# A fused two-block transformer kernel: rotary angles for 32 rates only, low-rank blocks multiplied with raw x, squares summed on TensorE, and the r product made to follow its operand by tiles

## The reference

```
hn = x * rsqrt(mean(x*x, features) + 1e-6) * g              # per token, g per feature
p  = hn @ w_in                                              # r, k, v, two low-rank blocks, and more
p  = p + (token_shift(p) - p) * mu                          # mix with the token before
r, k, v, wd, ad, gd = split(p)                              # wd, ad: 64 columns each; gd: 128
w  = -softplus(-(w0 + tanh(wd) @ w2)) - 0.5;  a = sigmoid(a0 + ad @ a2);  g = sigmoid(gd) @ g2
angle = position * 10000 ** (-i / 32), i = 0..31            # rotary: 32 rates, for retention later
```

## Time and profile before

| | us |
|---|---|
| median of 3 runs | 2716.07 (2714.88 to 2716.72) |
| the profiled execution: its time | 2714.77 |
| the profiled execution: its span in the trace | 2712.6 |
| PE busy, share of the span | 2498.0 (92%) |
| DVE busy | 1208.9 (45%) |
| POOL busy | 741.4 (27%) |
| ACT busy | 717.4 (26%) |

### The profile page before, as it was taken

The page is one execution under the profiler, slowest core; times in us unless marked ns, Lnnn a source line. Parts: engine busy times, 40 slices in busy tenths (PEclk is TensorE's granted clock), DMA queues, the critical chain, the costliest instruction groups (busy, mean ns, idle before and its releaser), DMA issues.

```text
span 2712.6 us, 33501 instructions
## 1 busy us (share of the span) xinstructions
PE 2498.0 (92%) x12944; PEld 1998.6 (74%) x12944; DVE 1208.9 (45%) x1324; ACT 717.4 (26%) x1013; POOL 741.4 (27%) x375
## 2 busy tenths in 40 slices
PE   3999999999999997998996999999999995999896
PEld 3787877877887886877784788888878774777674
DVE  7543263335335344554516444444421417536633
ACT  3422222131222222223213222222222323014421
POOL 3321221131212110003334333333334443222132
PEclk9999999999999998998996999999999996999988
DMA  2111111121121116434511111111132220111011
GB/s 115 62 55 55 63 49 52 47 71 47 48 70 47 60 50 202 137 105 145 196 47 62 62 46 46 46 46 46 46 132 93 93 93 13 45 48 47 24 35 65
DMA packets 48787, 191.02 MB, mean 70 GB/s; under 512 B 5424, under 2 KB 6192, under 8 KB 47408
## 3 DMA queue, kind: packets, MB, share of 16 engines
q1 hardware_dynamic: 28224, 102.77, 11.4%
q10 hardware_dynamic: 20464, 86.76, 8.8%
HBM read 152.81 MB, written 36.70 MB: 70 GB/s over the span
## 4 chain that ended last, share of the span: by engine, by line
PE 82%; DVE 9%; DVEq 4%; ACT 2%; issue 1%; DMA 1%; POOL 0%; ACTq 0%; POOLq 0%; SPq 0%
PE psg L338 11%; PE psg L334 11%; PE psg L339 11%; PE psg L437 5%; PE psg L442 5%; PE psg L444 5%; PE psg L750 1%; PE psa L402 1%; PE psg L754 1%; PE psg L753 1%; PE psa L533 1%; PE psg L363 1%; PE psg L811 1%; PE psb L522 1%; PE psg L806 1%
## 5 line engine op out<-in xcount | busy, mean ns | idle before, releaser
L271 POOL CAST whi<-wraw 128x1024 fp32r<-128x1024 f32 (+1 forms) x152 | 175.0, 1151 | 1711.3 <-PE psg L437 619.2
L334 PE MATMUL psg<-xhi,whi 128*128 128x512 f32 x1280 | 506.8, 396 | 8.5 <-DVE fg L1204 3.8
L338 PE MATMUL psg<-xlo,whi 128*128 128x512 f32 x1280 | 509.0, 398 | 0.0
L339 PE MATMUL psg<-xhi,wlo 128*128 128x512 f32 x1280 | 505.0, 395 | 0.0
L273 POOL TENSOR_TENSOR wlo<-wraw,whi 128x1024 fp32r<-128x1024 f32 (+1 forms) x152 | 403.4, 2654 | 21.8
L334 PEld LDWEIGHTS psg<-xhi,whi 128*128 128x128 f32 x1280 | 240.5, 188 | 72.1 <-issue 5.9
L338 PEld LDWEIGHTS psg<-xlo,whi 128*128 128x128 f32 x1280 | 240.7, 188 | 58.1 <-issue 1.0
L339 PEld LDWEIGHTS psg<-xhi,wlo 128*128 128x128 f32 x1280 | 240.7, 188 | 57.0
L444 PE MATMUL psg<-xhi,wlo 128*128 128x512 f32 x640 | 265.8, 415 | 0.0
L442 PE MATMUL psg<-xlo,whi 128*128 128x512 f32 x640 | 265.6, 415 | 0.0
L437 PE MATMUL psg<-xhi,whi 128*128 128x512 f32 x640 | 265.4, 415 | 0.0
(11 more groups left out here) (415 smaller groups left out, 4332.9 us busy)
## 6 DMA issues: line engine op xcount, KB each, us to landing
wraw<-w SPq DMA_DIRECT2D x196, 512.0 KB, 3.5
later_scratch<-stage ACTq DMA_DIRECT2D x40, 512.0 KB, 2.7
xres<-xt ACTq DMA_DIRECT2D x4, 1024.0 KB, 11.1
RV<-later_scratch ACTq DMA_DIRECT2D x4, 1024.0 KB, 12.9
RG<-later_scratch ACTq DMA_DIRECT2D x4, 1024.0 KB, 5.1
later_scratch<-rstage ACTq DMA_DIRECT2D x8, 512.0 KB, 2.7
mgr<-later_scratch ACTq DMA_DIRECT2D x8, 512.0 KB, 3.6
mgt<-later_scratch ACTq DMA_DIRECT2D x8, 512.0 KB, 4.4
```

Source lines behind the costliest of these rows:

```text
L271: pool.tensor_copy(whi[:, u, 0:width], wraw[:, u, 0:width])
L334: mm = pe.matmul(psg[b][:, cols], whi[:, slot, w_cols], rhs_hi(k, cols), start=(k == 0), stop=False)
L338: pe.matmul(psg[b][:, cols], whi[:, slot, w_cols], rhs_lo(k, cols), start=False, stop=False)
L339: mm = pe.matmul(psg[b][:, cols], wlo[:, slot, w_cols], rhs_hi(k, cols), start=False, stop=(k == kts - 1))
```

## The change: what it does

- The angles are computed on [128, 256] tiles: 32 rates on 32 partitions, four quarters of the tokens on the four groups of partitions. DVE computes both angle tables ahead of all else, and ACT takes four sines [128, 256] before it touches x. The table in DRAM is written by four transfers and read back by four in place of one and one.
- Positions (a quarter as many) and parameters are loaded ahead of x.
- ACT makes `rhi`, the high half of x times the gain g, as the tiles land, DVE makes `rlo`. The two low-rank blocks are multiplied with these, without the root.
- The squares (ACT makes five, DVE three) are no longer added up by POOL and DVE. TensorE sums each tile's square over partitions and accumulates in PSUM (`square_sums`: the eight one-column matmuls, once for each of the eight tiles).
- Once the root has been spread, DVE copies it to `xrs`, multiplies each low-rank block out of PSUM by it (`low_scaled`), and scales and splits x as before.
- The r product of each pair takes the operand tile by tile with both halves of a tile together, and waits for each tile (`norm_split`).

The diff, cut to its core:

```diff
@@ -45,7 +45,11 @@
-SPLIT_BEFORE = {"yrw": 0, "yret": 4, "merged": 12, "cat": 20}
+SPLIT_BEFORE = {"x": 0, "yrw": 8, "yret": 12, "merged": 20, "cat": 28}
+SQUARED_BY_DVE = (2, 4, 6)
+QT = T // 4
@@ -147,13 +151,16 @@
-        pa_sq = tiles("pa_sq", 8, [P, 2, T])
-        pa_acc = tiles("pa_acc", 10, [P, T])
...
+        pa_sq = tiles("pa_sq", 8, [P, 4, T])
+        pa_tmp = tiles("pa_tmp", 8, [P, 2, T])
+        pa_rstd, xrs = tiles("pa_rstd", 10, [P, T]), tiles("xrs", 11, [P, T])
+        rlo, rhi = tiles("rlo", 12, [P, KT, T], F32R), tiles("rhi", 20, [P, KT, T], F32R)
+        PRE = [tiles("pre_low0", 12, [P, T]), tiles("pre_low1", 13, [P, T])]
+        LOW = [tiles("low0", 14, [P, T]), tiles("low1", 15, [P, T])]
@@ -287,15 +294,6 @@
-            pool.memset(pp[:, 14:15], 1.0)
-            pool.memset(pa_acc[:, :], 0.0)
-            pool.drain()
...
-            for j in range(KT // 2):
-                pool.drain()
-                pool.wait_ge(sem("a_sq"), j + 1)
-                pool.tensor_tensor(pa_acc[:, :], pa_acc[:, :], pa_sq[:, j % 2, :], ALU.add
-                                   ).then_inc(sem("a_added"), 1)
@@ -415,11 +413,54 @@
+            def low_part(u, k, begins=False):
+                for half in range(2):
+                    cols = slice(half * HALF, (half + 1) * HALF)
+                    w_cols = slice(k * P, (k + 1) * P)
+                    mm = pe.matmul(psg[u][:, cols], whi[:, u, w_cols], rhi[:, k, cols], start=(k == 0), stop=False)
+                    if begins and half == 0:
+                        mm.then_inc(w_used, 1)
+                    pe.matmul(psg[u][:, cols], whi[:, u, w_cols], rlo[:, k, cols], start=False, stop=False)
+                    mm = pe.matmul(psg[u][:, cols], wlo[:, u, w_cols], rhi[:, k, cols],
+                                   start=False, stop=(k == KT - 1))
+                if k == KT - 1:
+                    mm.then_inc(g_full, 1)
+            def square_sums(k):
+                if k in SQUARED_BY_DVE:
+                    pe.wait_ge(sem("normed"), SQUARED_BY_DVE.index(k) + 1)
+                else:
+                    pe.wait_ge(sem("a_sq"), k + 1 - sum(j < k for j in SQUARED_BY_DVE))
+                for c in range(NB):
+                    mm = pe.matmul(psa[:, 0, c:c + 1], pa_sq[:, k % 4, c * P:c * P + P], pp[:, 14:15],
+                                   start=(k == 0 and c == 0), stop=(k == KT - 1 and c == NB - 1))
+                mm.then_inc(sem("a_added") if k < KT - 1 else sem("norm_tot"), 1)
+            def low_ready(u):
+                pe.wait_ge(w_ready, B_LORA + u + 3)
+                pe.wait_ge(g_free[u], T_LORA // 2 + 1)
+            low_ready(0)
+            pe.wait_ge(sem("pp_ready"), 1)
+            for k in range(KT):
+                pe.wait_ge(sem("op_split"), SPLIT_BEFORE["x"] + k + 1)
+                low_part(0, k, begins=(k == 0))
+                if k == KT // 2:
+                    low_ready(1)
+                if k >= KT // 2:
+                    low_part(1, k - KT // 2)
+                if k:
+                    square_sums(k - 1)
+            square_sums(KT - 1)
+            for k in range(KT // 2, KT - 2):
+                low_part(1, k, begins=(k == KT // 2))
...
-            norm_factor(pa_acc, pa_rstd, "a")
-            streamed(B_LORA, T_LORA, sem("norm_split"), 0, early=4)
+            pe.wait_ge(sem("norm_exp"), NORM["a"] + 1)
+            spread(pa_rstd).then_inc(sem("norm_rep"), 1)
+            for k in range(KT - 2, KT):
+                low_part(1, k)
@@ -453,7 +494,21 @@
-                for j in range(3):
+                pe.wait_ge(w_ready, B_RW + RW_B * i + 3)
+                pe.wait_ge(g_free[0], 8 * i + 2)
+                for k in range(KT):
+                    pe.wait_ge(sem("norm_split"), k + 1)
+                    w_cols = slice(k * P, (k + 1) * P)
+                    for half in range(2):
+                        cols = slice(half * HALF, (half + 1) * HALF)
+                        mm = pe.matmul(psg[0][:, cols], whi[:, 0, w_cols], xhi[:, k, cols], start=(k == 0), stop=False)
+                        if half == 0 and k == 0:
+                            mm.then_inc(w_used, 1)
+                        pe.matmul(psg[0][:, cols], whi[:, 0, w_cols], xlo[:, k, cols], start=False, stop=False)
+                        mm = pe.matmul(psg[0][:, cols], wlo[:, 0, w_cols], xhi[:, k, cols],
+                                       start=False, stop=(k == KT - 1))
+                mm.then_inc(g_full, 1)
+                for j in range(1, 3):
@@ -899,17 +954,21 @@
...
+            def normed(j):
+                stt(pa_tmp[:, j % 2, :], xres[:, j, :], par_col("g_mix_pre", j), flat(psa), MUL, MUL
+                    ).then_inc(sem("normed"), 1)
+            def normed_low(j):
+                v.wait_ge(sem("norm_high"), j + 1)
+                tt(xlo[:, j, :], pa_tmp[:, j % 2, :], xhi[:, j, :].bitcast(F32), SUB).then_inc(sem("norm_split"), 1)
+                v.drain()
+            def low_scaled(u):
+                v.wait_ge(g_full, u + 1)
+                tt(PRE[u][:, :], psg[u][:, :], xrs[:, :], MUL).then_inc(g_free[u], 1)
@@ -942,33 +1004,41 @@
-            v.wait_ge(sem("a_added"), KT // 2 + 2)
-            for j in range(KT // 2, KT):
-                v.drain()
-                v.wait_ge(sem("a_sq"), j + 1)
-                tt(pa_acc[:, :], pa_acc[:, :], pa_sq[:, j % 2, :], ADD).then_inc(sem("a_added"), 1)
+            v.drain()
+            turns(0.25, rot[:, 1, :])
+            for j in range(KT):
+                v.wait_ge(sem("op_high"), SPLIT_BEFORE["x"] + j + 1)
+                stt(rlo[:, j, :], xres[:, j, :], par_col("g_mix_pre", j), rhi[:, j, :].bitcast(F32), MUL, SUB
+                    ).then_inc(sem("op_split"), 1)
+                if j in SQUARED_BY_DVE:
+                    if j >= 4:
+                        v.wait_ge(sem("a_added"), j - 3)
+                    tt(pa_sq[:, j % 4, :], xres[:, j, :], xres[:, j, :], MUL).then_inc(sem("normed"), 1)
...
-            split_normed("x", xres, "g_mix_pre", pa_rstd, pa_tmp)
+            v.tensor_copy(xrs[:, :], flat(psa))
+            v.drain()
+            low_scaled(0)
+            v.wait_ge(sem("rot_stored"), 64)
+            for j in range(KT):
+                normed(j)
+                if j:
+                    normed_low(j - 1)
+                if j == 3:
+                    low_scaled(1)
+            normed_low(KT - 1)
...
+                stt(LOW[u][:, 1:T], PRE[u][:, 0:T - 1], par_col("mu_low", u), LOW[u][:, 1:T], MUL, ADD
+                    ).then_inc(sem("low_mix"), 1)
@@ -1387,45 +1457,49 @@
...
+            s.wait_ge(sem("angle"), 2)
+            act(rot[:, 2, :], rot[:, 0, :], ACT.Sin)
+            act(rot[:, 3, :], rot[:, 1, :], ACT.Sin)
+            act(rot[:, 0, :], rot[:, 0, :], ACT.Sin, scale=-1.0)
+            act(rot[:, 1, :], rot[:, 1, :], ACT.Sin).then_inc(sem("sincos"), 1)
...
-                s.wait_ge(sem("a_added"), j + 1)
-                act(pa_sq[:, j % 2, :], xres[:, j, :], SQ).then_inc(sem("a_sq"), 1)
+                act(rhi[:, j, :], xres[:, j, :], IDN, scale=par_col("g_mix_pre", j)).then_inc(sem("op_high"), 1)
+                if j not in SQUARED_BY_DVE:
+                    if j >= 4:
+                        s.wait_ge(sem("a_added"), j - 3)
+                    act(pa_sq[:, j % 4, :], xres[:, j, :], SQ).then_inc(sem("a_sq"), 1)
+            s.wait_ge(sem("sincos"), 1)
+            for q in range(4):
+                s.dma_start(rot_d[:, :, q * QT:(q + 1) * QT], rot[q * 32:q * 32 + 32, :, :]
+                            ).then_inc(sem("rot_stored"), 16)
...
+            for u in range(2):
+                s.wait_ge(g_free[u], 2)
+                act(LOW[u][:, :], PRE[u][:, :], IDN, scale=pp[:, 10 + u:11 + u]).then_inc(sem("low_a"), 1)
+            s.wait_ge(sem("low_mix"), 1)
+            act(LOW[0][0:CH, :], LOW[0][0:CH, :], ACT.Tanh)
+            s.wait_ge(sem("low_mix"), 2)
+            act(LOW[1][:, :], LOW[1][:, :], SIG)
...
-            s.wait_ge(sem("rot_stored"), 16)
+            s.wait_ge(sem("rot_stored"), 64)
@@ -1545,7 +1619,9 @@
-            s.dma_start(rott[:, :, :], rot_d).then_inc(sem("rot_in"), 16)
+            for r in range(4):
+                s.dma_start(rott[r * 32:r * 32 + 32, :, :], rot_d[:, 2 * (r % 2):2 * (r % 2) + 2, :]
+                            ).then_inc(sem("rot_in"), 16)
@@ -1871,7 +1947,7 @@
-    given = {"xt": feature_major(f["x"][0]), "pos": np.broadcast_to(f["positions"], (P, T)), "w": w, "par": par,
+    given = {"xt": feature_major(f["x"][0]), "pos": np.repeat(f["positions"].reshape(4, QT), P // 4, axis=0), "w": w, "par": par,
...

```

63 lines of the change are left out of this document (18 added, 45 removed).

## The result

| | us |
|---|---|
| changed kernel, median of 20 runs | 2723.69 (2716.41 to 2733.42) |
| kernel before, measured beside it, 20 runs | 2714.32 |
| ratio | 1.0038, interval 1.0026 to 1.0050 |
| profiled execution: time, span | 2733.42, 2731.4 |

The change costs 9.4 us by the medians and 10.3 by the ratio; 2728.5 was predicted, with 2716 to 2742 as the range. The profiled execution is the slowest of the 20, 18.8 us of span above that of before, so I read single stages in it and not its end.

A forecast was written before the change was run, and what follows sets the result against it. TensorE's work in program order was taken to bound the opening, then DVE's read of r to hold back v: v's start +11.2, clock +0.8, rotary table +0.7, sum +12.7 on 2714.77, given as 2728.5 us; range 2716 to 2742.

The forecast's parts named there:

- the wait for r's PSUM ahead of v: Before v's product, TensorE was to stand still for 3.0 us until ACT and DVE had read r.
- The first product: Opening: TensorE was to start its first product at 18.0 us (15.6 to 19.5), after angles, sines and first halves.
- the delay by POOL: Opening: POOL's split of the first weight block was to delay DVE's angle work by 2.4 us.
- The price of a sum: Opening: each token sum was to cost TensorE 1.84 us, eight of them 14.7 in place of 3.5.
- The third rival: Opening: narrow matmuls' weight loads vanish under dense ones, a sum costs 0.4 us, total 2705.7; chance 0.07.
- I take a fall at six of the eight: 9.0: Opening: TensorE's clock was to drop to 1.2 GHz after six of eight token sums, costing 9.0 us.
- N: Time when the root's spread ends on TensorE; forecast 66.4 us, against 40.07 in the kernel before.
- the first rival: Opening: the clock holds after the sums, the spread ends at 57.4 us, total 2719.8; chance 0.22.
- the 1.8 allowed for POOL's split ahead of the spread: Before the spread: POOL's next split was to delay DVE's expanding copy of the root, from 54.5 to 56.3 us.
- N to v, 41.0: From the spread's end to the start of v's product: 41.0 us through DVE's and ACT's chain, putting v at 107.4.
- The clock at that wait, 0.8: At v: the 3.0 us stop might cost a fall of TensorE's clock, half of 1.5, so 0.8 us.
- The rotary table, 0.7: Retention stage: three more issues for the table's four reads ahead of loads DVE awaits, 0 to 1.6 us, taken as 0.7.

The follow-up runs named there:

- run 1: Changed kernel with six of the eight token sums cut from eight matmuls to one; 2711.68 us, ratio to the kernel before 0.9992.
- run 2: Changed kernel, but DVE adds the squares of two neighbouring tiles, four token sums in place of eight; 2718.56 us, ratio to the kernel before 1.0024.
- run 4: Changed kernel with angles computed after DVE's work on the raw tiles and sines after ACT's; 2718.53 us, ratio to the kernel before 1.0019.
- run 6: Changed kernel with the rotary table stored by sixteen transfers and read back by one in place of four; 2718.77 us, ratio to the kernel before 1.0017.
- run 3: Changed kernel with DVE's clearing of SC moved up beside ACT's tanh and sigmoid; 2715.99 us, ratio to the kernel before 1.0018.
- run 8: Changed kernel with the edits of run 3, run 4 and run 6 together; 2708.41 us, ratio to the kernel before 0.9990.
- run 9: Run 8 with POOL adding up the squares again and one token sum in place of eight; 2726.28 us, ratio to the kernel before 1.0058.
- run 10: Run 8 with ACT's root ahead of the sixteen stores, issued three behind each high half, and the second angle table later; 2709.49 us, ratio to before 0.9989.
- run 11: Run 10 with DVE adding the squares of two neighbouring tiles before TensorE sums them; 2706.75 us, ratio to the kernel before 0.9974.
- run 12: Run 11 with the rotary table stored by four transfers and read by two of 64 partitions; 2732.47 us, ratio to the kernel before 1.0076.
- run 7: Kernel before with only the rotary table's read cut into four transfers of 32 partitions; 2716.32 us, ratio to the kernel before 1.0017.

## Why the prediction was right, and where it was not

The size was right, 12.7 predicted and 9.4 to 10.3 measured, but by luck: v came 5.3 sooner than predicted, since the clock held, and two terms behind it came 4.4 dearer, and the two errors nearly cancelled. What bounds the opening and the wait for r's PSUM ahead of v were predicted rightly.

- **The first product**: 19.4 against 18.0. The parameters landed at 5.2 where 4.0 was the estimate, which is most of it; the delay by POOL was 2.1 (2.4).
- **The price of a sum**: right at 1.84, eight in a row of work on TensorE; run 1 shows it. The third rival (cheap sums) is out: sixteen records take 1.84, two 0.28. The time that it rests on in the Trainium skill (TensorE: Matmul & The Clock Gate, section "Back-to-back issue gap") is there the gap of an isolated matmul; of a stream in which each matmul has a weight load of its own the same section says that this gap is too short for few columns, and the trace agrees.
- **"I take a fall at six of the eight: 9.0"** is the step that failed. The clock held behind the six single sums and fell once, at the only two that stood next to each other, for 3.0. The argument that eight sums among 1.4 to 2.8 us of products are denser in sums than anything before counted sums; in the traces 1.4 of products between two sums were enough. What else the falls in the kernel before hung on stays open. N was 60.2, near the first rival's 57.4, whose mechanism is the true one, with a start 1.4 later, that one fall of 3.0, and without the 1.8 allowed for POOL's split ahead of the spread (57.4 + 1.4 + 3.0 - 1.8 = 60.0).
- **N to v, 41.0**: right, 41.9, its wait included (3.74 for 3.0), and by the mechanism named: the read of r behind `pp_ready`.
- **The clock at that wait, 0.8**: mis-sized, 2.5. Behind a stop of 3.7 to 4.1 v's products ran slow in all five traces that have it (the changed kernel, runs 1, 2 and 4 from the first matmul on, run 6 from its sixth matmul), behind one of 0.5 to 0.6 in none (runs 3 and 8 to 12).
- **The rotary table, 0.7**: mis-sized, 3.4 by the traces. I had counted issues, and held that the queue was full of older bytes; the bytes themselves moved at half the rate.

The sum with measured terms: 5.9 + 2.5 + 3.4 = 11.8, against 11.2 + 0.8 + 0.7. The interval of the ratio, 7.1 to 13.6 us, holds both.

## What to carry to other kernels

Put narrow sums one by one between dense products (six of them cost no clock here, though a single one can), and price each by a row of the same form in a trace; but keep no two of them together. Ask of every short stop of TensorE whether its clock will fall behind it: here that added 2.4 to a stop of 3.7. Before blaming what an engine does ahead of a result, look whether anyone waited for that result (runs 8 and 10). Move a table over all 128 partitions in one transfer, and look at GB/s beside the DMA share before calling a queue full.

## What was not expected of the hardware

- One cut in the partitions of a 1 MB read costs 3 to 5 us of the stage behind it (runs 6 and 7), and two reads whose pattern has two blocks as its outermost dimension cost 31 (run 12; the cause is not shown).
- ACT issues a store of 32 partitions in 0.65 us (16 in 10.35), and its next instruction stands behind them: in run 9 that is over half of TensorE's wait, in runs 6 and 8 nobody waited for it.
- DVE's two-operand work on 1024 columns takes 3.4 in place of 1.22 beside a split or an addition on POOL (runs 9 and 11).
